# Strassen block products for fourteen projections of each gated layer, gates through exp and ln, last expert group written out

## What is computed

```
h = rms_norm(x, norm_pre);  proj = h @ w_in        # 256 x 1024 @ 1024 x (18*512 + 8 + 5*1024)
sb_q sb_k sb_v sb_z | ml_q ml_k ml_v ml_o ml_z | gm_u gm_v gm_z | rt_q rt_k rt_v rt_z | xa_q xa_z   # 512 wide each
y_sb = stick_breaking(sb_q, sb_k, sb_v);             y_xa = memory_attention(xa_q, mem_k, mem_v)
y_ml = head_norm(mlstm(silu(conv(ml_q)), silu(conv(ml_k)), ml_v, ...)) * sigmoid(ml_o)
y_gm = gelu(gm_u) * mixed(gelu(gm_v));               y_rt = head_norm(retention(rot(rt_q), rot(rt_k), rt_v))
ys = [y_n * silu(z_n) for the five branches n]
merged = sum_n sigmoid(gates_n) * (ys_n @ w_up_n);   x = x + rms_norm(merged @ w_out, norm_post)
```

## Time and profile before

| | us |
|---|---|
| runs (3): median, lowest, highest | 2224.58, 2219.55, 2225.68 |
| the profiled execution: its own time | 2226.01 |
| its span in the trace | 2224.2 |
| PE busy, DVE busy, ACT busy | 1914.0, 949.4, 371.6 |

### The profile page before, as it was taken

The page is one execution under the profiler, slowest core; times in us unless marked ns, Lnnn a source line. Parts: engine busy times, 40 slices in busy tenths (PEclk is TensorE's granted clock), DMA queues, the critical chain, the costliest instruction groups (busy, mean ns, idle before and its releaser), DMA issues. The chain is left out here.

```text
span 2224.2 us, 24226 instructions
## 1 busy us (share of the span) xinstructions
PE 1914.0 (86%) x10184; PEld 1153.7 (52%) x10184; DVE 949.4 (43%) x1518; ACT 371.6 (17%) x751; POOL 0.2 (0%) x4
## 2 busy tenths in 40 slices
PE   8999977767766667767668999999999999999998
PEld 5687733323323333322223787774446787874445
DVE  6858522212212112121223254487752254577762
ACT  1123300000000000000001222122333222123322
POOL 0000000000000000000000000000000000000000
PEclk9999998888889898887888999999999999999999
DMA  7222899999999999999997344445532433336430
GB/s 299 84 76 101 334 431 432 433 429 432 430 431 429 433 431 428 429 430 432 431 433 291 114 152 170 137 159 188 209 117 103 152 151 142 136 119 246 155 148 19
DMA packets 31926, 594.77 MB, mean 267 GB/s; under 512 B 3918, under 2 KB 5200, under 8 KB 7512
## 3 DMA queue, kind: packets, MB, share of 16 engines
q1 hardware_dynamic: 29912, 584.31, 63.9%
q10 hardware_dynamic: 1920, 9.09, 1.3%
HBM read 590.22 MB, written 1.06 MB: 266 GB/s over the span
## 5 line engine op out<-in xcount | busy, mean ns | idle before, releaser
L2019 PE MATMUL ps<-ring,arena 128*32 128x512 f32 x2032 | 291.6, 728 | 150.5 <-DMA ring<-in_w_experts 141.8
L612 PE MATMUL ps<-arena,ring 128*128 128x256 f32 x1792 | 399.9, 378 | 1.0 <-DVE arena L1163 0.8
L612 PEld LDWEIGHTS ps<-arena,ring 128*128 128x128 f32 x1792 | 333.7, 189 | 50.0 <-issue 3.4
L806 PE MATMUL ps<-ring,arena 128*128 128x512 f32 x656 | 286.4, 592 | 0.0
L2019 PEld LDWEIGHTS ps<-ring,arena 128*32 128x32 f32 x2032 | 73.3, 130 | 352.0 <-issue 224.6
L2051 PE MATMUL ps<-ring,arena 128*32 128x256 f32 x2016 | 154.2, 458 | 61.2 <-DMA ring<-in_w_experts 60.5
L806 PEld LDWEIGHTS ps<-ring,arena 128*128 128x128 f32 x656 | 124.5, 190 | 155.1 <-issue 155.0
L2680 DVE COPY arena<-ps 128x256 f32<-128x256 f32 x64 | 27.2, 425 | 277.6 <-PE ps L2051 277.6
L2051 PEld LDWEIGHTS ps<-ring,arena 128*32 128x32 f32 x2016 | 71.4, 128 | 130.1 <-issue 78.9
L1975 PE MATMUL ps<-arena 128*128 128x256 f32 x256 | 81.5, 445 | 34.9 <-DVE arena L2680 34.9
L2670 DVE TENSOR_TENSOR arena<-arena,ps 128x512 f32<-128x512 f32 x16 | 11.0, 689 | 228.7 <-PE ps L2019 228.7
(11 more groups left out here) (445 smaller groups left out, 2061.2 us busy)
## 6 DMA issues: line engine op xcount, KB each, us to landing
ring<-in_w_experts SPq DMA_DIRECT2D x90, 4096.0 KB, 23.4
ring<-in_w_layers SPq DMA_DIRECT2D x64, 2048.0 KB, 7.7
ring<-in_w_experts SPq DMA_DIRECT2D x10, 2048.0 KB, 9.4
ring<-in_w_first SPq DMA_DIRECT2D x9, 2048.0 KB, 7.9
early<-in_w_layers SPq DMA_DIRECT2D x6, 2048.0 KB, 8.4
arena<-in_w_mem SPq DMA_DIRECT2D x4, 2048.0 KB, 20.6
ring<-in_w_first SPq DMA_DIRECT2D x4, 512.0 KB, 7.8
early<-in_w_experts SPq DMA_DIRECT2D x1, 2048.0 KB, 25.1
```

The lines of the kernel that those rows point to most:

```text
L612: last = pe.matmul(ps[:, j % 2, 0:SEQ], t[:, s, k, :], lhs[:, k, :], start=(k == 0), stop=(k == KD - 1))
L806: last = pe.matmul(ps[:, bank, :], lhs[:, k, :], rhs[:, k, :], start=(first and k == 0), stop=(k == n - 1), skip_group_check=True)
L2019: last = pe.matmul(ps[CAP * e:CAP * (e + 1), v // 4, :], xg[:, (v % 4) * 2 + k, CAP * e:CAP * (e + 1)], w[:, k, e, :], start=(v % 4 == 0 a ...
```

## The change

Fourteen projections (all but the four by token) become seven block products each. With the normalised tokens x as 2 x 2 blocks (half the features by half the tokens) and the weights as 2 x 2 blocks b11, b12, b21, b22 (two k halves by two output halves), a product is 8 matmuls of 128x128 weights against 128 tokens. Products 1, 6, 5 and 3 of a projection pile up in one PSUM bank and ACT copies each sum to its quarter of the target; products 2, 7 and 4 use a second bank, and DVE adds them (`add_quarter`). DVE forms the four weight sums in the ring slot and in `total` (`first_sums`, `late_block`; 1024 elements each). The order of products over two projections is 1, 2, 3 of the last, 6, 4 of the last, 7, 5.

So products 3 and 4 of a projection come after products 1, 2 and 6 of the next, and SP's wait for a used-up unit is now a wait for product 4 (`unit_end`). The order of the projections changes too: sb_z first, gm_z last, rt_v before gm_u.

The gates are computed on whole projections of 1024 elements: ACT exp, DVE min, ACT ln and exp, DVE multiply. gm_z lies in the place of ml_v (ring slot 3) and its gate in that of ml_o, which reaches into slot 4. Hence SP's new wait for `gated_y` of gm_z before it loads merge+4 and, behind that, merge+3.

In block one the last group of experts leaves the loop; its last four units are loaded one by one, the last in two halves.

```diff
 # layers_sync
-                        job_done(sp, plan.job_ends[i - RING2] - 1)
+                        unit_end(i - RING2)
...
+                after_product(sp, l, "rt_z", 3)
+                after_gated(sp, l, "ml_z")
+                layer_unit(sp, plan.merge_unit + 1)
...
+                after_gated(sp, l, "gm_z")
                 sp.wait_ge(sem("rt_h"), NH * (l + 1))
                 layer_unit(sp, plan.merge_unit + 4)
                 sp.wait_ge(sem("rt_y"), l + 1)
                 layer_unit(sp, plan.merge_unit + 3)
 # layers_pe
+                def halved(name, p):
...
+                    if p == 2:
...
+                        elif i >= 2:
+                            after_add(pe, l, HALVED[i - 2], 4)
+                    if p == 6:
+                        after_copy(pe, l, name, 1)
+                        after_sum(pe, l, name, 2)
...
+                    for s in range(2):
+                        for k in range(4):
+                            last = pe.matmul(ps[:, bank, s * P:(s + 1) * P], lhs[:, s, k, :], rhs[:, k, :],
 # layers_dve
+                def first_sums(name):
...
+                    unit_loaded(dve, u)
+                    dve.tensor_tensor(b12, b22, b12, ALU.subtract).then_inc(sem("w_sum"), 1)
...
+                    dve.tensor_tensor(total, b12, b11, ALU.add).then_inc(sem("w_sum"), 1)
...
+                def halved(name, p):
...
+                    if p in (2, 5, 4):
+                        add_quarter(name, p)
+                    if p == 2:
+                        late_block(name, 1)
...
+                    if p == 3 and i + 1 < len(HALVED):
+                        late_block(HALVED[i + 1], 2)
+                    if p == 6 and i + 1 < len(HALVED):
+                        first_sums(HALVED[i + 1])
...
 # layers_dve, branch 0 of the merge
                     if b == 0:
+                        gate_times("rt_z")
+                        after_gated(dve, l, "rt_z")
                         head_scale(rt_q, "rth", y_all[:, 3], "rt_y")
...
+                    if b == 0:
+                        gate_bound("gm_z")
...
                     if b == 0:
+                        gate_times("gm_z")
 # sync, after the loop over the groups
+            for v in range(8, 12):
...
+                sp.wait_ge(sem("unit_free"), last_group * 12 + v + 1)
```

More of the change, by code:

```diff
@@ L68 @@
 SLOT2 = (2, 0, 1)
-UNIT_GROUPS = [("gm_v",), ("sb_v",), ("sb_q",), ("sb_k",), ("mem_k",), ("sb_z", "xa_q"), ("mem_v",), ("xa_z",), ("ml_q", "ml_k"),
-               ("ml_v",), ("ml_o",), ("ml_z",), ("rt_q", "rt_k"), ("rt_v",), ("gm_u",), ("rt_z", "gm_z")]
-MEM_GROUPS = (("mem_k",), ("mem_v",))
+CHAIN = ("sb_z", "sb_q", "sb_k", "xa_q", "xa_z", "ml_q", "ml_k", "ml_o", "ml_v", "ml_z", "rt_q", "rt_k", "rt_z", "rt_v", "gm_u", "gm_z")
+UNITS = ("gm_v", "sb_v") + CHAIN
+MEM_UNITS = ("mem_k", "mem_v")
 ON_TOKENS = ("sb_v", "ml_v", "rt_v", "gm_v")
@@ L80, with chain_steps @@
 SHARED_W = 28300
+def chain_steps():
+    steps, last = [], None
+    for name in CHAIN:
+        if name in ON_TOKENS:
+            steps += [(name, "t0"), (name, "t1")]
+            continue
+        steps += [(name, 1), (name, 2)] + ([(last, 3)] if last else []) + [(name, 6)] + ([(last, 4)] if last else []) + [(name, 7), (name, 5)]
+        last = name
+    return steps + [(last, 3), (last, 4)]
+STEPS = chain_steps()
+HALVED = [n for n in CHAIN if n not in ON_TOKENS]
+PRODUCTS = [s for s in STEPS if s[0] in HALVED]
+COPIES = [s for s in PRODUCTS if s[1] in (1, 6, 5, 3)]
+ADDS = [s for s in PRODUCTS if s[1] in (2, 5, 4)]
+TOKEN_JOBS = [(n, i) for n in ("gm_v", "sb_v", "ml_v", "rt_v") for i in range(2)]
+GATES = ("sb_z", "xa_z", "ml_o", "ml_z", "rt_z", "gm_z")
+GATED = ("sb_z", "xa_z", "ml_z", "rt_z", "gm_z")
 class Pack:
@@ L448, in build_program @@
         assert lw.at <= r_three
+        gm_zt = spare[:, 8 * (SEQ + 4):8 * (SEQ + 4) + 4 * SEQ].rearrange("p (a b) -> p a b", b=SEQ)
+        le = Layout(early[:, :])
+        x_early = [le.take(4, P) for _ in range(4)]
+        gate_tmp = le.take(4, SEQ)
+        assert le.at <= WSLOT
         lw = Layout(spare)
@@ L485, in build_program @@
         post = y_all.rearrange("p a b c -> p (a b c)")[:, 0:KD * SEQ].rearrange("p (a b) -> p a b", b=SEQ)
[L486 to L487 removed]
+        target = {"sb_z": y_all[:, 0], "sb_q": sb_q, "sb_k": sb_k, "xa_q": xa_q, "xa_z": y_all[:, 4],
+                  "ml_q": wide[:, 0:4, 3:3 + SEQ], "ml_k": wide[:, 4:8, 3:3 + SEQ], "ml_o": ml_o, "ml_z": y_all[:, 1],
+                  "rt_q": rt_q, "rt_k": rt_k, "rt_z": y_all[:, 3], "gm_u": gm_u, "gm_z": gm_zt}
+        gate_at = {"sb_z": gate_tmp, "xa_z": gate_tmp, "ml_o": ml_o, "ml_z": gate_tmp, "rt_z": ml_o, "gm_z": ml_o}
         def P2(l, name, i=0, rows=P, row=0):
@@ L729, in layers_pe @@
-                for k in range(KD // 2):
-                    for half in range(2):
-                        for gate in range(2):
-                            at = FG * (2 * half + gate)
-                            last = pe.matmul(ps[at:at + FG, 2, 0:SEQ], w_if[:, 2 * k + half, FG * gate:FG * (gate + 1)], an[:, 2 * k + half, :],
-                                             start=(k == 0), stop=(k == KD // 2 - 1))
-                last.then_inc(sem("mg_ps"), 1)
-                on_tokens("ml_v", 1)
@@ new lines, in layers_act, with run, gate_exp @@
+                chain = iter(STEPS)
+                def run(n):
+                    for name, p in itertools.islice(chain, n):
+                        if name in ON_TOKENS:
+                            m = ("t0", "t1").index(p)
+                            take(name, m, (ml_v if name == "ml_v" else rt_v)[:, m, :])
+                        else:
+                            halved(name, p)
+                def gate_exp(name):
+                    whole(act, l, name)
+                    at = GATED.index(name) if name in GATED else 0
+                    if name in GATED[1:]:
+                        after_gated(act, l, GATED[at - 1])
+                    act.activation(xr(gate_at[name]), xr(target[name]), ACT.Exp, scale=-1.0).then_inc(sem("gate_x"), 1)
```

639 lines of the change are left out of this document (399 added, 240 removed).

## The result

| | before | changed |
|---|---|---|
| median of 4 runs, us | 2222.86 | 2264.92 |
| lowest to highest | 2219.55 to 2225.68 | 2259.63 to 2268.28 |
| span of the profiled execution | 2224.2 | 2261.4 |
| PE busy, DVE busy, ACT busy | 1914.0, 949.4, 371.6 | 1884.3, 1035.5, 407.3 |

The change makes the kernel slower: ratio 1.0188, 95% interval 1.0175 to 1.0200, or 42 us. I had forecast 2279, 54 us above the median then shown, with a range of 2225 to 2310: the direction was right and the size 12 us too large. PE is busy 29.7 us less, DVE 86 us more.

What follows compares the result with a forecast made beforehand. PE's own work was taken to bound the layers, transfers the experts. Terms of +27.7 us a layer, +55.4 for two, less 1.4 for the experts, gave +54.0: 2280 profiled, 2279 as median, range 2225 to 2310.

Steps and rivals of the forecast that it cites:

- PE's arithmetic: Projections: 112 passes of 128 columns at 114 ns replace 64 at 215.8 ns; 14.7 us a layer saved over fourteen projections.
- short waits: Wait behind the mixing sums partly filled by a second head's logits, plus small head-loop waits; 2 us a layer off.
- late weights, mlstm stretch: Projections ml_z and rt_q: PE waits for late weight loads and for DVE and ACT work behind them; +10 us a layer.
- late weights, retention stretch: First retention head, its weights and gm_z: PE waits for the late rotation, DVE work and gm_z's unit; +14.4 us a layer.
- merge: Branch 0: late gm_z gate delays two weight loads, DVE's sums and the add PE needs; +15 us a layer.
- clock: PE runs slower after long stalls: 2 us each in retention and merge, 1 for the rest; +5 us a layer.
- both ends of the forecast's sum: Totals 2233 (110 ns, least waits, 1 for the clock) and 2303 (old 16 us turned copy, 17 in the merge).
- the experts: Last expert group: its unit 8, loaded alone, comes some 4 us earlier, so 1.4 us comes off.
- The bound at 110 ns: Faster pass time in the projections, kept for the range; 21 us a layer saved.
- The first rival: Layers: loads and gates come before PE needs them, so waits are hidden and PE's saving stands; 2190 us, chance 0.10.

Runs made afterwards that it cites:

- the early gate: Changed kernel with ACT's exp of gm_z and DVE's gate products for rt_z and gm_z done earlier in the merge; 2241.68 us.
- the last kernel: Changed kernel with retention-stretch DVE work reordered, products 3 and 4 ahead of jobs by token, gm_z's gate, both merge adds and ml_v's centring earlier; 2180.62 us.
- both adds moved: Changed kernel with the adds of g22 (and its bound) and u22 in merge branch 0 ahead of DVE's sums of branch 1; 2247.57 us.
- the run with one add moved: Changed kernel with only the add of g22 in merge branch 0 ahead of DVE's sums of branch 1; 2263.7 us.

## Why the prediction was right, and where it was off

The forecast was right in direction, in mechanism and, within its range, in size: 42 us where it said 54 by its sum. By its steps, a layer (layer 0, layer 1):

| term | forecast | measured |
|---|---|---|
| PE's arithmetic | -14.7 | -18.3 |
| short waits | -2 | -1.6 |
| late weights, mlstm stretch | +10 | +9.1, +9.4 |
| late weights, retention stretch | +14.4 | +12.4, +10.9 |
| merge | +15 | +14.7, +14.7 |
| clock | +5 | +9.5, +7.6 |
| sum | +27.7 | +25.8, +22.7 |

The clock's entry is what the other entries leave of the stage times, small waits of under 1 us included.

One reading of the forecast was off at the start: layer 1 is not the same within 1%, since its merge stage lasted 222.5 us where that of layer 0 lasted 216.7; PE's busy time in it is the same, 212.9. And both ends of the forecast's sum, 2233 and 2303, leave out the 1.4 us of the experts: they should read 2231 and 2302. Nothing hangs on either.

*PE's arithmetic* was mis-sized. I took 114 ns from the gather, whose row of 32 passes lasts 3.81 us; a row of 32 new passes lasts 3.73, the pitch is 111.6, and 1568 passes make 3.7 us a layer of the difference. The bound at 110 ns was nearer than my value.

*The mlstm stretch* came out in two of three terms: 4.35 for the unit of rt_q (forecast 4.1), 2.52 for ACT's copy (2), 2.22 for the centring (4.0). *The retention stretch* came out in its main terms: 8.07 and 6.74 at the first head (7), 3.03 for gm_z's unit (2.9); but 1.27 for the weights (3.4), and nothing at the add behind gm_z's unit (1.1). The copies were issued at 1430.7 and the rotation began at 1437.6, 6.9 us later (6.5).

*The merge* came out within 0.2 us at every step in layer 0: the gate at T+27.3 (27.3), both loads there at T+39.8 (39.8), PE ready at T+32.8 (32.6), the add done at T+47.4 (47.5). That this chain is the cause is shown by the early gate and by the two runs with moved adds, and it was not the whole of what stood behind the sums: the gathers did too.

*The clock* was under-sized, 5 for 7.6 to 9.5. In layer 0 the timeline has slow rows behind five of the waits: 1.7 us over their pitch behind the 4.35, 1.7 behind the 2.22, 1.9 behind the 8.07, 2.0 behind the 3.03 and 3.0 behind the 14.66. I had counted 2 each in the retention stretch and in the merge and 1 us for the rest. Layer 1 has no slow row behind its wait of 2.23 us, and 1.9 us less in the table. The same passes took PE 987.4 us in the layers of the changed kernel and 969.0 in the last kernel, which has none of these waits. So some 18 us in two layers go with the waits, though no run tested the clock's part by itself.

*The experts* were off by 3 us: 4.4 in the profiles, 4.6 in the runs of that part alone, for 1.4. I had counted the wait for one pair; with the units loaded one by one, the half clock behind that wait went too: the first two of the four rows of 32 down passes took 3.64 and 3.44 us before and take 1.93 each in the changed kernel.

The errors of the pitch (7 us in two layers), of the retention stretch (5.5), of the mlstm stretch (1.5) and of the experts (3) made the forecast too high, that of the clock (7) too low. So the 12 us by which it missed are in part luck: without the clock's error it would have missed by 19. The first rival (waits hidden, 2190) was no description of this kernel, but of what it can be: with the waits taken away the runs gave 2180.6. The mechanism by which the change lost was the order of work around it, and that is shown and not only argued, since the same instructions in another order gain 1.9% on the kernel before, of which the last expert group has 0.2. The block products without the new gates were not run.

## What to carry over

Where an engine is the bound and is never idle, price a change to it in two parts: what its own work gains, and for every wait that the new order adds, what stands behind the waiting instruction on its engine, down to the next one that the bound engine needs. If the balance is bad only by the second part, move the waits before giving up the first: freeing a buffer early (here product 4 ahead of a long job) and issuing no add behind sums that wait for a load turned 42 us lost into 42 us won. And when an edit aimed at one wait brings nothing, read which wait stands there now; twice here it was the neighbour of the one that was moved.

## What the runs showed of the hardware that I had not expected

An f32 pass with 128 columns keeps a pitch of 111.6 ns while each of its weight loads lasts 192 to 198 ns in the trace. So consecutive loads overlap each other as well as the passes, also when every pass has weights of its own, for 1568 passes a layer.

Whether the clock falls behind a wait cannot be read from the wait alone. Behind 3.03 us (gm_z's unit), 48 passes took 7.50 where 5.52 is usual, at a granted clock of 0.77, and behind 14.66 us, 8 took 6.64 in place of 3.60, at 0.55: the lower level, 1.2 GHz, for a while. But behind 2.6 us in branch 1 (both adds moved), 16 passes took 7.13, at 1.00: full clock, 2.4 GHz.

The same wait at the same place can do either. At ACT's copy in ml_z, in code that is the same in both kernels, 16 passes took 2.05 us behind 2.52 and 2.56 us idle in the changed kernel (1.00), and 3.63 and 3.68 behind 2.42 and 2.50 us in the run with one add moved (0.68 over 5.2 us). And in layer 0 of the changed kernel a wait of 2.22 us, 9 us after one of 4.35, had a slow stretch behind it (0.68):

```profile
1371.01 5.46 PE L711 MATMUL ps<-arena,ring 128*128 128x128 f32 x32 [4.35 <-DMA ring<-in_w_layers]
...
1380.01 2.56 PE L711 MATMUL ps<-early,ring 128*128 128x128 f32 x16 [2.22 <-DVE ring L1546]
1382.37 3.11 PE L711 MATMUL ps<-early,arena 128*128 128x128 f32 x16
```

In layer 1 the same pair, 4.57 and 2.23 us, was followed by slow passes only behind the first: behind the second, 16 passes took 2.05 us and the next 16 took 1.95. What decides it these runs do not show. A forecast should give such a wait a chance of the loss and not a fixed price.

The start of the experts varies by 4.3 us over ten profiles (258.6 to 262.9) and lies at 265.5 in that of before. It begins with PE's wait for the first weights, 8.8 us in the profile of before and 6.2 in that of the changed kernel. A difference of a few us between two profiles should be read by stages, and held against the medians, before it is given to a change.
